# A mixture-of-experts decoder block on one core: expert passes of 96 token rows instead of 128

## The reference, cut to what matters

```
top_val, top_idx = lax.top_k(hf @ w_router + b_router, 4)   # 512 tokens, 2048 (token, expert) pairs
weights = softmax(top_val)
for each expert e, on the rows of the tokens that chose it:
    gate, up = split(xb @ w_gate_up[e] + b_gate_up[e])       # 1024 -> 2 x 1024
    act = (clip(up) + 1) * min(gate, 7) * sigmoid(1.702 * gate)
    y  += weight * (act @ w_down[e] + b_down[e])             # 1024 -> 1024
```

## Time and profile before

| | us |
|---|---|
| median of 3 runs | 1864.67 (1862.64 to 1866.17) |
| span of the profiled execution, first to last instruction | 1852.6 |
| median less that span | 12.1 |
| PE busy | 1811.6 (98%) |
| DVE busy | 1409.8 (76%) |
| ACT busy | 1177.7 (64%) |
| POOL busy | 351.6 (19%) |
| moved by DMA | 503.71 MB, mean 272 GB/s |

### The profile page before, as it was taken

How to read it: one execution, slowest core, us unless ns; L and a number is a source line. 1 busy time by engine, 2 the same in 40 slices (tenths; PEclk the granted TensorE clock), 3 DMA queues, 4 the chain that set the end, 5 groups by cost and what they waited for, 6 DMA issues and landing times.

```text
span 1852.6 us, 25122 instructions
## 1 busy us (share of the span) xinstructions
PE 1811.6 (98%) x8997; PEld 1504.8 (81%) x8997; DVE 1409.8 (76%) x1027; ACT 1177.7 (64%) x936; POOL 351.6 (19%) x327
## 2 busy tenths in 40 slices
PE   6999999999999999999999999999999999999997
PEld 6888888678889878888888888888888888888876
DVE  4576676563334689889889899889888988988974
ACT  4655465342223577777777777777777777777774
POOL 5123324530000412111111111211211111111000
PEclk8999999999999999999999999999999999999999
DMA  6444343342337299999999999999999999999941
GB/s 182 115 106 103 114 125 101 110 131 81 110 115 280 68 405 363 365 376 368 365 371 374 366 372 375 372 368 384 364 368 382 364 368 377 364 370 367 376 162 46
DMA packets 152888, 503.71 MB, mean 272 GB/s; under 512 B 15290, under 2 KB 75362, under 8 KB 119204
## 3 DMA queue, kind: packets, MB, share of 16 engines
q1 hardware_dynamic: 140916, 478.10, 69.4%
q0 software_dynamic: 11872, 24.83, 5.7%
q10 hardware_dynamic: 48, 0.07, 0.0%
HBM read 493.28 MB, written 25.90 MB: 280 GB/s over the span
## 4 chain that ended last, share of the span: by engine, by line
PE 85%; DVE 4%; POOL 3%; ACT 3%; issue 2%; DMA 1%; POOLq 0%; DVEq 0%; SPq 0%; ACTq 0%
PE gu_ps L2098 24%; PE dn_ps L2113 12%; PE gu_ps L2102 12%; PE gu_ps L1866 7%; PE gu_ps L1868 7%; PE gu_ps L1867 7%; PE dn_ps L2119 6%; PE et_ps L2084 3%; PE gu_ps L2089 1%; PE gu_ps L1888 1%; PE dn_ps L2267 1%; ACT w_hi L897 1%; POOL win L800 1%; PE gu_ps L2171 1%; POOL dx L786 1%
## 5 line engine op out<-in xcount | busy, mean ns | idle before, releaser
L1682 DVE TENSOR_TENSOR split_l<-ring,split_h 128x2048 fp32r<-128x2048 f32 x384 | 868.1, 2288 | 101.0 <-ACT split_h L1163 98.2
L1163 ACT ACTIVATE split_h<-ring 128x2048 fp32r<-128x2048 f32 x384 | 727.6, 1916 | 154.5 <-PE gu_ps L2102 121.8
L2098 PE MATMUL gu_ps<-split_h,xgT_h 128*128 128x512 f32 x992 | 274.7, 399 | 0.7 <-DVE xgT_l L1688 0.7
L2102 PE MATMUL gu_ps<-split_l,xgT_h 128*128 128x512 f32 x992 | 265.5, 389 | 0.0
L2098 PE MATMUL gu_ps<-split_h,xgT_l 128*128 128x512 f32 x992 | 265.4, 389 | 0.0
L2098 PEld LDWEIGHTS gu_ps<-split_h,xgT_l 128*128 128x128 f32 x992 | 186.2, 188 | 39.4
L2102 PEld LDWEIGHTS gu_ps<-split_l,xgT_h 128*128 128x128 f32 x992 | 186.2, 188 | 39.1
L2098 PEld LDWEIGHTS gu_ps<-split_h,xgT_h 128*128 128x128 f32 x992 | 184.1, 188 | 39.9 <-issue 1.2
L1342 DVE TENSOR_TENSOR w_lo<-w_raw,w_hi 128x2048 fp32r<-128x2048 f32 (+1 forms) x45 | 103.1, 2291 | 143.6 <-ACT w_hi L897 130.2
L813 POOL COPY icur<-slots 128x1 int32 (+1 forms) x31 | 52.5, 1695 | 690.4 <-PE et_ps L2084 690.4
L2113 PE MATMUL dn_ps<-split_h,actT_h 128*128 128x512 f32 x496 | 155.6, 395 | 0.0
(11 more groups left out here) (359 smaller groups left out, 2630.7 us busy)
## 6 DMA issues: line engine op xcount, KB each, us to landing
ring<-in_w_gate_up SPq DMA_DIRECT2D x256, 1024.0 KB, 7.3
ring<-in_w_down SPq DMA_DIRECT2D x128, 1024.0 KB, 8.3
w_raw<-in_w_in SPq DMA_DIRECT2D x28, 1024.0 KB, 5.8
arow<-acum_rows POOLq DMA_DIRECT2D x16, 512.0 KB, 6.5
w_raw<-in_w_ssd_out SPq DMA_DIRECT2D x8, 1024.0 KB, 5.9
w_raw<-in_w_in SPq DMA_DIRECT2D x9, 512.0 KB, 6.3
w_raw<-in_w_mix_out SPq DMA_DIRECT2D x4, 1024.0 KB, 8.6
wpg<-in_w_ple_gate SPq DMA_DIRECT2D x2, 2048.0 KB, 20.3
```

The costliest lines, as they stand in the source:

```text
L1163: a.activation(split_h[s % SPLIT][:, :], ring[s % RING][:, :], ACT.Copy).then_inc(hi_done, 1)
L1682: v.tensor_tensor(split_l[s % SPLIT][:, :], ring[s % RING][:, :], split_h[s % SPLIT][:, :].bitcast(F32), ALU.subtract).then_inc(lo_done, 1)
L2098: t.matmul(gu_ps[:, b * 512:b * 512 + 512], x[:, k, :], split_h[s][:, b * 512:b * 512 + 512], start=False, stop=False)
L2102: o = t.matmul(gu_ps[:, b * 512:b * 512 + 512], xgT_h[:, k, :], split_l[s][:, b * 512:b * 512 + 512], start=False, stop=k == KD - 1)
```

## The change

Everything that was sized by 128 token rows in the expert stage becomes ROWS = 96: the slot table has 96 slots per expert and pass, and PASSES = 6 (512 / 96, rounded up). So 6 fill DMAs of 96 rows stand where 4 of 128 rows stood, and passes 1 to 5 run if the largest count is above 96. The stationary operands of the expert matmuls have 96 columns, the transposes turn blocks of 96 rows (the identity they stream has 96 columns), the evictions read 96 partitions or 96 slots per block, and gathers and scatters name 96 rows. The moving columns (512) and the number of instructions of a pass stay. In PSUM the blocks of a transpose still begin every 128 columns.

```diff
-PASSES = SEQ // P
+ROWS = 96
+PASSES = -(-SEQ // ROWS)
...
-        xg = here("xg", [P, DM], F32)
+        xg = here("xg", [ROWS, DM], F32)
...
-        xgT_h = here("xgT_h", [P, KD, P], F32R)
-        xgT_l = here("xgT_l", [P, KD, P], F32R)
+        xgT_h = here("xgT_h", [P, KD, ROWS], F32R)
+        xgT_l = here("xgT_l", [P, KD, ROWS], F32R)
...
-            with eng.If(rows > P):
+            with eng.If(rows > ROWS):
...
             for j in range(PASSES):
-                pool.dma_start(slot_rows[j], slots[:, :, :].rearrange("p e f -> p (e f)")).then_inc(filled, 16)
+                pool.dma_start(slot_rows[j], slots[0:ROWS, :, :].rearrange("p e f -> p (e f)")).then_inc(filled, 16)
             pool.sem_inc(consts_done, 1)
...
-                    gather(m0, slots[:, 0:1, 0], k0 + 1)
+                    gather(m0, slots[0:ROWS, 0:1, 0], k0 + 1)
...
-                a.activation(dst[:, :, :], et_ps[:, :].rearrange("p (k t) -> p k t", k=KD), ACT.Copy, scale=scale
+                a.activation(dst[:, :, :], et_ps[:, :].rearrange("p (k t) -> p k t", k=KD)[:, :, 0:ROWS], ACT.Copy, scale=scale
...
-                a.activation(y_sb[:, :], ps[:, :], ACT.Copy, scale=wcur[:, 0:1]).then_inc(y_evac, 1)
+                a.activation(y_sb[:, :], ps[0:ROWS, :], ACT.Copy, scale=wcur[:, 0:1]).then_inc(y_evac, 1)
...
-                        o = t.matmul(et_ps[:, k * P:k * P + P], X[:, c, k * P:k * P + P], first[c][:, :],
+                        o = t.matmul(et_ps[:, k * P:k * P + ROWS], X[:, c, k * P:k * P + P], first[c][:, :],
...
-                    o = t.transpose(et_ps[:, k * P:k * P + P], blocks[:, k * P:k * P + P], ident[:, :])
+                    o = t.transpose(et_ps[:, k * P:k * P + ROWS], blocks[:, k * P:k * P + P], ident[0:ROWS, 0:ROWS])
...
-                t.matmul(out, sel[:, bass.ds(e, 1)].to_broadcast([3 * NE, P]), bparts[:, col:col + 512],
+                t.matmul(out, sel[:, bass.ds(e, 1)].to_broadcast([3 * NE, ROWS]), bparts[:, col:col + 512],
...
-                        t.matmul(gu_ps[:, b * 512:b * 512 + 512], x[:, k, :], split_h[s][:, b * 512:b * 512 + 512],
+                        t.matmul(gu_ps[0:ROWS, b * 512:b * 512 + 512], x[:, k, :], split_h[s][:, b * 512:b * 512 + 512],
...
-                            t.matmul(ps[:, b * 512:b * 512 + 512], x[:, 2 * r + k, :],
+                            t.matmul(ps[0:ROWS, b * 512:b * 512 + 512], x[:, 2 * r + k, :],
```

More of the change, by code:

```diff
@@ L333, in program @@
         oh = [here(f"oh{i}", [P, TOPK, NE], F32) for i in range(2)]
-        first = [here(f"first{i}", [P, P], F32) for i in (2, 3)]
+        first = [here(f"first{i}", [P, ROWS], F32) for i in (2, 3)]
         assert top[0] <= (nc.sbuf_usable_end - CH * DM * 4) // 64 * 64
@@ L374, in program @@
         top[0] = upper_off
[L375 removed]
+        first.insert(0, here("first0", [P, ROWS], F32))
         top[0] = par1_off
[L377 removed]
+        first.insert(1, here("first1", [P, ROWS], F32))
         top[0] = arena
@@ L396, in program @@
         share3 = here("share3", [P, CH, 3, NE], F32)
-        place = here("place", [P, SEQ], F32R)
-        idxf = here("idxf", [P, 1], F32)
+        place = here("place", [ROWS, SEQ], F32R)
+        idxf = here("idxf", [ROWS, 1], F32)
         assert top[0] <= xgT_off
@@ L852, in one_pass @@
                 alone(pool)
-                weigh(slots[:, 0:1, 1].bitcast(F32))
+                weigh(slots[0:ROWS, 0:1, 1].bitcast(F32))
                 if isinstance(j, int):
@@ L856, in one_pass @@
                 else:
-                    gather(m0, slots[:, 0:1, 0], k0 + 1)
+                    gather(m0, slots[0:ROWS, 0:1, 0], k0 + 1)
                 pool.wait_ge(et_done, t0 + 1)
-                gather(m0 + 1, slots[:, 1:2, 0], k0 + 2)
+                gather(m0 + 1, slots[0:ROWS, 1:2, 0], k0 + 2)
                 pool.wait_ge(et_done, t0 + 2)
-                gather(m0 + 2, slots[:, 2:3, 0], k0 + 3)
+                gather(m0 + 2, slots[0:ROWS, 2:3, 0], k0 + 3)
                 if isinstance(j, int):
@@ L866, in one_pass @@
                     pool.wait_ge(et_done, t0 + e * 2 + 4)
-                    gather(m0 + e + 3, slots[:, bass.ds(e + 3, 1), 0], k0 + e * 2 + 4)
-                    scatter(j * NE + e, slots[:, bass.ds(e, 1), 0], k0 + e * 2 + 5, slots[:, bass.ds(e + 1, 1), 1].bitcast(F32))
+                    gather(m0 + e + 3, slots[0:ROWS, bass.ds(e + 3, 1), 0], k0 + e * 2 + 4)
+                    scatter(j * NE + e, slots[0:ROWS, bass.ds(e, 1), 0], k0 + e * 2 + 5, slots[0:ROWS, bass.ds(e + 1, 1), 1].bitcast(F32))
                 for e in range(NE - 3, NE - 1):
-                    scatter(j * NE + e, slots[:, e:e + 1, 0], k0 + NE + e + 1, slots[:, e + 1:e + 2, 1].bitcast(F32))
+                    scatter(j * NE + e, slots[0:ROWS, e:e + 1, 0], k0 + NE + e + 1, slots[0:ROWS, e + 1:e + 2, 1].bitcast(F32))
             pool.wait_ge(filled, 16 * PASSES)
@@ L880, in _ @@
                 pool.wait_ge(et_done, j * PASS_T)
-                scatter(j * NE - 1, slots[:, NE - 1:NE, 0], j * 2 * NE)
+                scatter(j * NE - 1, slots[0:ROWS, NE - 1:NE, 0], j * 2 * NE)
                 one_pass(j)
@@ L1791, in _ @@
                                   ).then_inc(share_done, 1)
-                v.scalar_tensor_tensor(y_l[:, at], last_ps[:, at], wcur[:, 0:1], y_h[:, at].bitcast(F32), ALU.mult,
+                v.scalar_tensor_tensor(y_l[:, at], last_ps[0:ROWS, at], wcur[:, 0:1], y_h[:, at].bitcast(F32), ALU.mult,
                                        ALU.subtract).then_inc(y_low, 1)
-            step(v.tensor_copy(idxf[:, :], slots[:, NE - 1:NE, 0]))
-            v.tensor_scalar(place[:, :], tokrow[:, :], idxf[:, 0:1], None, ALU.is_equal).then_inc(placed, 1)
+            step(v.tensor_copy(idxf[:, :], slots[0:ROWS, NE - 1:NE, 0]))
+            v.tensor_scalar(place[:, :], tokrow[0:ROWS, :], idxf[:, 0:1], None, ALU.is_equal).then_inc(placed, 1)
             dve.wait_ge(share_high, 1)
@@ L2132, in gate_up_bias @@
                 for b in range(4):
-                    bias(gu_ps[:, b * 512:b * 512 + 512], e, b * 512)
+                    bias(gu_ps[0:ROWS, b * 512:b * 512 + 512], e, b * 512)
             def down_free(n):
```

53 lines of the change are left out of this document (27 added, 26 removed).

## The result

The changed kernel takes 1868.80 us (median of 11 runs, 1866.10 to 1874.23), the kernel before, run beside it, 1863.17 us (11 runs, 1862.53 to 1866.42). The ratio is 1.0028, with a 95% interval from 1.0020 to 1.0035.

The account below looks back on a forecast made before the run. PE's own instruction stream was taken to bound the kernel. Terms -13.6 (transposes) + 0.9 (bias) + 1.1 (start) - 1.0 (first gathered rows) - 0.5 (tail) = -13.1 us, giving 1851.6 us, range 1834 to 1858.

Parts of the forecast that it names:

- The expert matmuls: no change.: Expert stage, 4608 matmuls: fewer stationary columns leave the 0.227 us distance as it is; 0, bounds -37 us and 0.
- Rival C: At each of 4608 expert matmuls, a partly filled array's load no longer hides; 4.6 us per ns, 1898 us at 10; chance 0.04.
- the signs: In the changed timeline: L2102's four matmuls still 1.07 us, expert 0.43 us less; PE idle before mid-stage matmuls means forecast wrong.
- The transposes: the gain: Turns on PE, 504 transposes: streaming 96 identity columns instead of 128 saves 27 ns each, -13.6 us.
- Rival B: In the turns, transposes stay at 0.110 us because a 96-row block's load sets them: 1865.2 us; chance 0.08.
- The bias: Bias matmuls of each expert: the first selector load may be seen, 27 ns longer at 96 columns, +0.9 us.
- The start: Kernel start: two more fill DMAs issued ahead of consts_done delay PE's first work, +1.1 us (0 to 1.2).
- The row selection: Expert 0's 64 matmuls of L2050 stream 96 columns instead of 128 but are bound by the load: 0.
- the first gathered rows: PE's first waits in the expert stage: shorter gather -0.5 and shorter evictions of xgT's halves -0.5, together -1.0 us.
- The tail: Kernel end: the last scatter loses 32 empty slots, but PE idles only 0.53 us there, -0.5 us.
- One pass still does: Expert stage: the largest gather has 85 rows, below 96 slots, so no further passes of about 1130 us each start.
- The base: Whole kernel: profiled span of 1852.6 us, plus the 12.1 us by which the runs' median exceeds it.

Follow-up runs that it names:

- the wide kernel: Changed kernel with expert-matmul and bias stationary operands 128 columns wide again, turns, gathers and scatters at 96 rows: 1851.96 us, ratio 0.9939.
- the repeated run of before: The unchanged kernel profiled a second time with nothing changed: 1862.01 us, span 1860.3.
- the held kernels: Unchanged, changed or wide-operand kernels with 12 or all 16 of GpSimd's slot scatters held back, some with other edits: 1849.09 to 1868.30 us.
- the first trace of before: First profiled execution of the unchanged kernel, on which the prediction rests: span 1852.6 us.

## Why the prediction was wrong, by its steps

- **"The expert matmuls: no change."** This step failed. The term measured 15.4 us by the traces (0.48 x 32) and 16.8 by the medians, where the sum had 0. Rival C named the place and the price, with a break-even at 2.8 ns; it came at (33.56 - 33.08) / 144 = 3.3 ns, and got a chance of 0.04. The mechanism that C gave, a load that no longer hides, is not shown: the loads got shorter, from 188 to 161 ns, and at 134 ns (64 columns) the distance was that of 96. The evidence that I took against C was of another kind: transposes and small matmuls of 128 moving columns, 0.11 us apart. "Three rows" were two, and the full array's own. No row had a float32r stream of 512 columns with a narrow operand, and the upper bound was set by rows too far away; "0, the end that three rows support" should have been a bound of some nanoseconds on the slow side, where one nanosecond is worth 4.6 us. The argument from the shorter load shows only that nothing is won by it; it doesn't rule out a loss. Two of the signs show it: the four matmuls of L2102 last 1.08 to 1.09 us instead of 1.07, and the expert isn't shorter. The one named for a wrong forecast, idle time of PE, doesn't: PE stays busy without a gap while its matmuls get longer.
- **"The transposes: the gain", -13.6 us.** Right: 0.87 to 0.66 us for eight. By the stage of the wide kernel it is -11.7 us for the 62 turns between its first and last, 24 ns a transpose for the 27 of the forecast; the matmuls behind a turn give a little of it back. Rival B is out.
- **The bias, +0.9.** The load did grow as assumed, in the changed kernel's group by line

```profile
L2091 PEld LDWEIGHTS gu_ps<-bparts,sel x128: 118/122/123, 653.2 to 1743.5; 96*96 x120, 96*96 96x96 bf16 x8
```

  from 98 ns to 122 (median). Here the trace agrees with the Trainium skill, "TensorE: Matmul & The Clock Gate", section "Weight-path perf modes", which keeps the fast load for full 128-column operands that aren't fp32. But it stays hidden; the bias took 0.01 us less, not 0.03 more.
- **The start, +1.1 us.** +0.9 at the first transposes (10.38 to 11.29) and as much at the first projection, 21.39 to 22.30. Right.
- **The row selection, 0, and the first gathered rows, -1.0.** The 1.3 us wait for the gather is in neither the repeated run of before nor the changed kernel, so its -0.5 wasn't to be had. It isn't gone from all executions with the stall, though: the wide kernel waits 1.7 us there. The wait for xgT's halves is 0.5 us in the changed kernel, for 0.7 and 1.0 in the two executions of before: -0.2 to -0.5. The evictions behind it did shorten as forecast, from 1.03 to 0.81 us on ACT and from 1.21 to 0.96 on DVE.
- **The tail, -0.5.** From the last expert matmul to the end, 78.7 us in the changed kernel and 80.9 in the repeated run of before; in the wide and the held kernels 79.2 to 81.6, so the spread is as large as the effect. The last scatter took 9.5 us for 11.5. Not contradicted, not settled.
- **One pass still does**: right, the expert stage is one pass, 1087 us between the turns that mark it.
- **The base.** Adding 12.1 us to a span of 1852.6 gave the right median, but the 10 us were a stall that the profiled execution didn't have. It did no harm to the forecast only because the stall is there with the change as without it; that is luck.

The sum with the terms that the traces give: 15.4 (matmuls, 32 x 0.48) - 11.7 (turns) - 0.3 (bias, 32 x 0.01) + 0.9 (start) = +4.3 us, and the medians differ by +5.6. A part of the rest goes with the clock: of the 11 runs of the changed kernel only 3 had a mean granted clock of 0.993 or more, and they average 1866.9 us; 35 runs of the kernel before had it, over all rounds, and average 1862.9. That is +4.0 us at the same clock; near 0.990 it is +4.9 (7 and 20 runs).

## What to carry to other kernels

Treat the distance between matmuls in a saturated stream as a property of the exact shape, stationary columns included, and don't carry it over to a narrower operand: with 4608 of them, 3 ns decided the sign here. When fewer rows are in use, cut what streams (here the transposes' moving side), and leave the stationary operand at its full 128 columns; the spare columns cost nothing here (33.08 us an expert in the wide kernel too). Profile the unchanged kernel twice when its span and its median differ by more than the other kernels' do.

## What the runs showed of the hardware that I had not expected

- Narrower stationary operands make float32r matmuls with 512 moving columns slower: 33.08 us for 144 at 128 columns, 33.09 at 124, 33.38 at 112, 33.50 at 96, though the load falls from 188 to 161 ns. The stride is not what does it: the 33.50 have 512-byte strides, and with 384-byte ones it is 33.56.
- While GpSimd issued indirect scatters back to back (each 0.97 us, every 1.28), VectorE started 4.7 to 9.1 us late on a semaphore of TensorE in eight of nine traces, and ScalarE up to 4.3; in the changed kernel TensorE's own wait on VectorE was answered within 0.1 us. In the eight kernels that hold scatters back VectorE was never late there, but in four of them ScalarE waited 2.1 to 2.2 us ahead of the first gathered rows. By what path the scatters do it is open, and so is why the first trace of before was spared.
- GpSimd's indirect gather of 96 rows occupies it for 5.2 us where the one of 128 rows took about 1.1, in the changed kernel (the group of its line: shortest, median and longest in ns)

```profile
L818 POOL DMA_INDIRECT xg<-h_rows,icur x31: 993/5224/5227, 665.3 to 1705.3; - x31
```

  and 7.7 us in the wide one; the rows land a median of 12.8 and 14.8 us behind the issue, for 8.1. Why is open. In the middle of the stage TensorE waits for it in neither; ahead of the second expert's turn it waits 1.7 us in the wide one.
